# Norms of q and k: from the start of each mixing tile into the projections

## What is computed

```python
qkv, dn_conv_new = causal_conv(dn_qkv, dn_conv_prev, dn_conv_w)
qkv = jax.nn.silu(qkv)
q, k, v = jnp.split(qkv, [DN_QK_DIM, 2 * DN_QK_DIM], axis=-1)
q = l2_normalize(q.reshape(bsz, length, DN_HEADS, DN_HEAD_K)) * (DN_HEAD_K ** -0.5)
k = l2_normalize(k.reshape(bsz, length, DN_HEADS, DN_HEAD_K))
v = v.reshape(bsz, length, DN_HEADS, DN_HEAD_V)
beta = jax.nn.sigmoid(dn_b.astype(jnp.float32))
o, dn_s = run_segments(gated_delta_chunked, (q, k, v, g, beta), dn_s0, n_lead)
```

## Time and profile before

| | |
|---|---|
| three timed runs, us | 5544.49, 5547.06, 5552.38 (median 5547.06) |
| the profiled execution, us | 5531.47 |
| its span, first to last instruction, us | 5529.6 |
| mean granted clock of TensorE | 0.806 of full speed |
| busy share PE, DVE, POOL, ACT | 64%, 63%, 51%, 9% |
| HBM traffic | 278 GB/s over the span |
| A, B, C (from the first instruction of one stage to the next) | 0 to 284, 1036 to 1463, 2698 to 3237 us |
| openings of the mixing tiles 0 to 8 (L1492) | 292, 617, 1468, 1825, 2251, 3242, 3599, 4021, 4465 us |

### The profile page before, as it was taken

One profiled execution on the slowest core, in us unless ns is written; L12 is line 12 of the kernel. 1 busy time (PEld: TensorE's weight loads), 2 busy tenths in 40 slices (PEclk: granted clock), 3 DMA queues, 4 the chain that ended last, 5 costly groups with the idle time before them and its releaser, 6 DMA issues. The chain is left out here.

```text
span 5529.6 us, 50329 instructions
## 1 busy us (share of the span) xinstructions
PE 3563.1 (64%) x16620; PEld 2011.1 (36%) x16620; DVE 3470.3 (63%) x7379; ACT 472.4 (9%) x1615; POOL 2792.7 (51%) x2333
## 2 busy tenths in 40 slices
PE   6877366588886566576478888566656646566206
PEld 5564262244462452352133355154235222111001
DVE  3244995568554895676557644599568667685370
ACT  1110000011110000000021110000000000000000
POOL 1010465564443665775454433376577575425685
PEclk9988688699998778777699999777877866578558
DMA  4452468898767779889888756688989986759768
GB/s 165 132 177 101 176 218 295 308 369 295 279 208 297 263 248 361 330 312 343 295 326 302 277 189 231 250 296 277 362 320 322 347 306 225 277 199 371 258 216 304
DMA packets 467249, 1496.86 MB, mean 271 GB/s; under 512 B 60097, under 2 KB 122241, under 8 KB 454417
## 3 DMA queue, kind: packets, MB, share of 16 engines
q0 software_dynamic: 324864, 1141.04, 57.2%
q1 hardware_dynamic: 120912, 330.01, 16.2%
q10 hardware_dynamic: 21216, 22.60, 1.3%
HBM read 1480.07 MB, written 55.29 MB: 278 GB/s over the span
## 5 line engine op out<-in xcount | busy, mean ns | idle before, releaser
L1946 POOL DMA_INDIRECT e_ring<-peer_u,e_idx x1152 | 1462.2, 1269 | 1189.8 <-issue 515.1
L1946 POOL DMA_INDIRECT e_ring<-peer_v,e_idxT x1104 | 1190.6, 1078 | 1138.4 <-PE e_ff L2098 599.1
L1982 DVE CUSTOM_DVE_ANT_0 e_ring<-e_ring,e_x 128x1024 f32<-128x1024 f32 (+1 forms) x1152 | 1393.6, 1243 | 276.2 <-DMA e_ring<-peer_u,e_idx 269.7
L2098 PE MATMUL e_ff<-e_ring,e_strips 128*32 128x512 f32 x4416 | 756.8, 784 | 609.7 <-DMA e_ring<-peer_v,e_idxT 469.9
L349 PE MATMUL p_ps<-p_hT,p_w 128*128 128x256 f32 (+2 forms) x1728 | 568.8, 483 | 0.0
L2098 PEld LDWEIGHTS e_ff<-e_ring,e_strips 128*32 128x32 f32 x4416 | 165.1, 129 | 1097.7 <-issue 1094.6
L349 PEld LDWEIGHTS p_ps<-p_hT,p_w 128*128 128x128 f32 x1728 | 328.8, 195 | 205.6 <-issue 125.9
L1332 PE MATMUL bank<-wbuf,kqb 128*128 128x512 f32 (+1 forms) x576 | 302.1, 682 | 110.7 <-DMA wbuf<-w_out 110.6
L1184 PE MATMUL bank<-X,atp 128*128 128x128 f32 (+1 forms) x1632 | 240.9, 299 | 91.0 <-DVE XT L1525 58.9
L1365 PE MATMUL bank<-wbuf,kqb 128*128 128x512 f32 (+1 forms) x576 | 272.9, 623 | 20.8 <-DMA wbuf<-wc 20.7
L1193 PE MATMUL bank<-T,XT 128*128 128x128 f32 (+1 forms) x1344 | 209.8, 307 | 94.4 <-DVE T L1531 89.9
(11 more groups left out here) (323 smaller groups left out, 4147.7 us busy)
## 6 DMA issues: line engine op xcount, KB each, us to landing
p_w<-w_in SPq DMA_DIRECT2D x156, 512.0 KB, 3.6
wbuf<-w_out SPq DMA_DIRECT2D x72, 1024.0 KB
wbuf<-wc SPq DMA_DIRECT2D x72, 1024.0 KB
e_ring<-peer_u,e_idx POOLq DMA_INDIRECT x1152
e_ring<-peer_v,e_idxT POOLq DMA_INDIRECT x1104
rows<-p_tok SPq DMA_DIRECT2D x72, 192.0 KB
rows<-rows SPq DMA_DIRECT2D x8, 1280.0 KB, 9.0
z<-p_zs SPq DMA_DIRECT2D x32, 256.0 KB
```

Of the source, the lines that this page charges most:

```text
L1946: g.indirect_dma_start(out=self.ring[:, i % RING, :], out_offset=None, in_=table[:, :], in_offset=at, bounds_check=NEXP - 1, oob_is_err=Fa ...
L1982: v.tensor_tensor_reduce(out=self.ring[0:U, i, :], in0=self.ring[0:U, i, :], in1=self.x[0:U, :], scale=1.0, scalar=0.0, op0=ALU.mult, op1= ...
L2098: last = nc.tensor.matmul(self.ff[i][32 * j:32 * j + 32, :], self.strips[:, self.strip_of[t] % NSTRIP, j, 31 - s:63 - s], self.ring[:, sel ...
```

## The change

The sums of squares of the heads of q and k are taken in `project`, from the transposed blocks in `tok`, two blocks behind: at block j VectorE sums the squares of block j - 3 and squares block j - 2 (j from 2 to 18), ahead of the taps of block j. At block 20 it takes the root for all rows of the stage's tiles at once and writes three new groups of 16 columns beside the gates: `rq` (with the factor 1/8), `rk`, and `rkb` = rk times beta. The gates have 256 columns then instead of 208, and their store waits for `g_norms`. In `mix_tile` the squares, sums, root and scaling are gone; VectorE waits for the gates, makes kb from the raw k with `rkb`, waits for that, and then scales k and q in place. Nothing of the other engines' work is changed.

```diff
 for _n, _w in (("g", 2 * H), ("ncum", 2 * H), ("ecum", 2 * H), ("elast", 2 * H), ("beta", H), ("nbecum", H),
-               ("edl", H), ("dt", H), ("dtedl", H)):
+               ("edl", H), ("dt", H), ("dtedl", H), ("rq", H), ("rk", H), ("rkb", H)):
...
-                sp.wait_ge(S["g_done"], 1)
+                sp.wait_ge(S["g_norms"], 1)
...
+                squares = Chain(v, S["g_sq"])
+                squares.mark(v.memset(ssq[:], 1.0))
+
+                def squared(j):
+
+                    v.wait_ge(S["c_trevac"], NB * (j + 1))
+                    squares.sync()
+                    last = v.tensor_tensor(sq[:, 0:nf, :], tok[:, j % 2, 0:nf, :], tok[:, j % 2, 0:nf, :], ALU.mult)
+                    if packed:
+                        last = v.tensor_tensor(sq[0:PACK, nf, :], tok[0:PACK, j % 2, nf, :], tok[0:PACK, j % 2, nf, :], ALU.mult)
+                    squares.mark(last)
+
+                def summed(j):
+
+                    squares.sync()
+                    halves = lambda ap: ap.rearrange("p i (h d) -> p i h d", d=HD)
+                    last = v.tensor_reduce(out=ssq[:, 0:nf, 2 * j:2 * j + 2], in_=halves(sq[:, 0:nf, :]), axis=AX, op=ALU.add)
+                    if packed:
+                        last = v.tensor_reduce(out=ssq[0:PACK, nf, 2 * j:2 * j + 2], in_=sq[0:PACK, nf, :].rearrange("p (h d) -> p h d", d=HD),
+                                               axis=AX, op=ALU.add)
+                    squares.mark(last)
+
+                def norms():
+
+                    squares.sync()
+                    inverse_root(v, squares, ssq[:], ssx[:], ssw[:], ssq[:], 1.0, L2_EPS)
+                    v.wait_ge(S["g_done"], 1)
+                    v.tensor_scalar(F("rq"), ssq[:, :, 0:H], HD ** -0.5, None, ALU.mult)
+                    v.tensor_copy(F("rk"), ssq[:, :, H:2 * H])
+                    v.tensor_tensor(F("rkb"), ssq[:, :, H:2 * H], F("beta"), ALU.mult).then_inc(S["g_norms"], 1)
+
                 taps = Chain(v, S["c_taps"])
                 v.wait_ge(S["c_cst"], 32 if packed else 16)
                 for j in range(CT):
                     if j >= 2:
                         copy_out(j - 1)
+                    if 1 <= j - 2 < H + 1:
+                        summed(j - 3)
+                    if 0 <= j - 2 < H:
+                        squared(j - 2)
+                    if j == H + 4:
+                        norms()
                     v.wait_ge(S["c_evac"], j + 1)
...
                 v.wait_ge(S["qk_in"], 16)
-                c(tt(sq[0:R, :], q, q, ALU.mult))
-                c(v.tensor_reduce(out=B["ss"][0:R, 0:H], in_=heads(sq[0:R, :]), axis=AX, op=ALU.add))
-                c(tt(sq[0:R, :], k, k, ALU.mult))
-                c(v.tensor_reduce(out=B["ss"][0:R, H:2 * H], in_=heads(sq[0:R, :]), axis=AX, op=ALU.add))
+                v.wait_ge(S["gates_in"], 16)
                 at("norm")
-                root_of(B["rs"][0:R, :], B["ss"][0:R, :], 1.0, L2_EPS, 2 * H)
-                c(v.tensor_scalar(B["rs"][0:R, 0:H], B["rs"][0:R, 0:H], HD ** -0.5, None, ALU.mult))
-                tt(heads(q), heads(q), per_head(B["rs"][0:R, 0:H]), ALU.mult)
-                tt(heads(k), heads(k), per_head(B["rs"][0:R, H:2 * H]), ALU.mult).then_inc(S["qk_norm"], 1)
-                v.wait_ge(S["qk_norm"], 1)
-                v.wait_ge(S["gates_in"], 16)
-                tt(heads(kb[0:R]), heads(k), per_head(F("beta")[0:R]), ALU.mult).then_inc(S["kb"], 1)
+                tt(heads(kb[0:R]), heads(k), per_head(F("rkb")[0:R]), ALU.mult).then_inc(S["kb"], 1)
+                v.wait_ge(S["kb"], 1)
+                tt(heads(k), heads(k), per_head(F("rk")[0:R]), ALU.mult)
+                tt(heads(q), heads(q), per_head(F("rq")[0:R]), ALU.mult).then_inc(S["qk_norm"], 1)
```

More of the change, by code:

```diff
@@ L166, in project @@
         out = sb("p_out", [P, NT, NG])
+        sq, ssq, ssx, ssw = sb("p_sq", [P, NT, P]), *(sb(f"p_{n}", [P, NT, 2 * H]) for n in ("ssq", "ssx", "ssw"))
         ps = [ctx.enter_context(nc.psum_tensor(f"p_ps{i}", [P, 512], F32, allow_name_mangling=True)) for i in range(6)]
@@ L172, in project @@
                  "z_ws", "z_small", "z_mm", "z_silu", "z_st0", "z_st1", "z_st2",
-                 "g_in", "g_v", "g_mag", "g_e1", "g_p1", "g_ln", "g_decay", "g_sums", "g_last", "g_exp", "g_done", "g_store"] + [
+                 "g_in", "g_v", "g_mag", "g_e1", "g_p1", "g_ln", "g_decay", "g_sums", "g_last", "g_exp", "g_done", "g_store", "g_sq", "g_norms"] + [
                  f"w_in{i}" for i in range(NWR)]
@@ L928, in allocate_mix @@
             ("delta", [P, 512], F32), ("bct", [P, 4, P], F32), ("cb", [P, 2, P], F32),
-            ("ss", [P, 2 * H], F32), ("rs", [P, 2 * H], F32), ("root_x", [P, 2 * H], F32), ("root_w", [P, 2 * H], F32),
+            ("ss", [P, H], F32), ("rs", [P, H], F32), ("root_x", [P, H], F32), ("root_w", [P, H], F32),
             ("ssy", [P, 2], F32), ("stats", [P, 2, 6], F32), ("mv", [P, 4], F32),
```

## The result

The changed kernel is slower by 0.39% (ratio 1.0039, 95% interval 1.0025 to 1.0053; medians 5567.95 and 5547.26 us, 18 runs of each). A second measurement, beside other runs of the kernel before, gave 1.0033 (1.0015 to 1.0050; medians 5546.80 and 5534.17 us). So the change costs about 20 us by the ratios, and 20.7 and 12.6 us by the medians; the forecast was 9.4, 5556.5 us, "same". In brief: the projections cost in sum what the forecast said, though its terms for the clock missed both ways; tile 0 gained a little more than it said; and the other 8 to 12 us could not be placed.

What follows compares the result with a forecast made beforehand. No engine is full; a chain of stages with barriers bounds the kernel, each with its own last wait. Projections +15.0 less openings 5.6 gives +9.4 us on the 5547.06 median: 5556.5 us, range 5537 to 5568.

Steps and rivals of the forecast that it cites:

- What gates an opening: Mixing-tile openings: TensorE's first transposes wait for GpSimd's cast of `hidden` in six tiles (71.2 us), for kb only in tile 0.
- the last rival: Mixing tiles: the opening on VectorE heads every tile's chain, 64 us less and 15 more, 5498 us; chance 0.06.
- Tile 0: Opening of the first mixing tile, without gathers: TensorE starts at 300.5 in place of 305.08, gain 4.6 us.
- Tiles 1, 3, 6: Openings that begin with seven dots: `hidden` comes no sooner, masks gain 0.3 us each, 1.0 in all.
- The rival: Tiles 1, 3, 6: early dots hold back gathers and the cast, `hidden` later, +1 us each; chance 0.20.
- The projections: Squares and sums fit the slack of ordinary blocks; stalls at the root and block 17, with clock, cost 15.0 us.
- A: Projection for tiles 0 and 1, 256 columns: root 2.0 us over its slack plus 1.6 of clock, 3.6.
- B: Projection for tiles 2 to 4, 384 columns: 2.1 us at block 17 and 1.1 at the root, 3.2.
- C: Projection for tiles 5 to 8: 2.9 us stall plus 2.9 clock at block 17, 0.8 at the root, 6.6.
- Roots of B and C: At block 20 of these projections: 1.1 and 0.8 us over the slack, plus 1.6 of clock for one of the two.
- the projections hide it: Projections: the root's steps overlap more and no stall shows, only -5.6 us, 5541.5 us; chance 0.12.
- stalls and locks: Projections and tiles 1, 3, 6: each new idle lowers the clock, early dots delay `hidden`; +20.6 us, 5567.7 us; chance 0.20.

Runs made afterwards that it cites:

- Openings alone: New mixing-tile openings with the old projections, constants in place of the norms, against the kernel before: 1.0002, measured again 0.9981.
- the root behind the blocks: Changed kernel with the root and its three closing products behind the last block instead of at block 20: 1.0029 and 1.0016 against the kernel before.
- norms in A only: Kernel before with squares, sums and root (behind the blocks) in the first projection alone, new opening in tile 0 alone, 256 gate columns: 1.0002.

## Why the prediction missed

**What gates an opening: right.** The transposes of all tiles without token sums ahead still wait for `hidden`; kb went from the list of what ends the idle time. Openings alone measured 1.0002 and 0.9981, nowhere near the 64 us of the last rival.

**Tile 0: right, somewhat low.** TensorE starts 5.2 us sooner behind the tile's first load (4.6 forecast), and the tile is shorter by about as much: it took 319.6 us on average in twelve profiles of nine kernels with the new opening, 326.1 in four profiles of two kernels with the old one, 6.5 less. The size is loose: with the same old opening it took 327.4 and 328.1 us in the kernel before and 324.4 and 324.7 with the new projections, and another 2.7 us won at its opening brought nothing.

**Tiles 1, 3, 6: half right.** I took 0.3 us of gain each and left the lengthened gathers to a rival, because "early dots come one by one, as their rows land, with gathers between them". That step failed: dots and gathers did overlap, and the cast came 1.9, 1.4 and 1.3 us later in the changed kernel. The rival was right on the cast and wrong on what follows: VectorE's first masks came 0.8 to 1.8 us sooner all the same, and holding the dots back gained nothing. What all new openings of tiles 1 to 8 are worth is 5 us of cost, give or take 10; the forecast's gain of 1.0 lies inside. So this step had the overlap wrong, and no run shows that it cost time.

**The projections: right in sum and in the stalls, partly by luck in the clock.** Forecast 15.0 us; the stretches add up to 3.5 + 1.2 + 2.7 + 5.3 + 2.2 = 14.9 in the changed kernel and 1.9 + 1.1 + 2.7 + 5.7 + 2.2 = 13.6 in its second profile, against the first profile of before (A at block 20, B at 17 and 20, C at 17 and 20). The added idles were as forecast: 1.85, 1.04 and 0.53 us at the roots (2.0, 1.1 and 0.8), 2.25 and 3.04 at block 17 of B and C (2.1 and 2.9). What the clock added was not, and the misses cancelled.

A: 3.6 forecast, 3.5 and 1.9 seen (chain 1.85; the clock fell in one of the two). At block 17 of B the idle grew as forecast, but only 1.2 of it was left at block 19, since the slow products took 6.76 us instead of the 7.85 of before. Over more profiles the cost is larger: eight with B as before took 22.4 to 25.3 us for this stretch, nine with the squares 26.3 to 27.5, on average 2.7 more. C at block 17: 5.8 forecast, 5.3 to 5.9 seen. Roots of B and C: forecast 1.1 and 0.8, and 1.6 of clock for one of the two, 3.5; seen 2.7 and 2.2, the clock fell in both, 4.9. Over the seven profiles with a root at block 20 it fell in two in A, where the forecast counted on it, in five in B, and in all seven in C. This is the term that the record shows mis-sized: 1.6 for one of the two, in place of some 1.7 for each. Against the rival "the projections hide it" every kernel with the whole change in the projections speaks.

**The sum: too small, and why is only partly known.** The steps known to have failed are the clock behind the roots of B and C and the gathers held to lie between the dots. Neither accounts for the missing time: the first is offset by A and by block 17 of B, the second has no price in any run. 14.9 less 6.5 is 8.4 us, the forecast's 9.4; measured are 20 (0.36% as the mean of two measurements; 16.7 by the medians).

The whole stages A, B and C say what their blocks say: 1263.5 us in the four profiles with changed projections and root at block 20 in the first table, 1248.8 in the four with the old ones, 14.7. With 5 us (give or take 10) in tiles 1 to 8 that makes 13, against 14 to 29 and 8 to 28 us by the two timed measurements. So the term that may have been mis-sized is tiles 1 to 8, set at -1.0; I cannot show it.

The same gap stands elsewhere by the ratios: with the root behind the blocks the profiles leave +1.1, +5.6 and -6.5, nothing in sum, and the times were 1.0029 and 1.0016; the five measurements of kernels with a shorter tile 0 and projections that cost nothing should have lain near 0.9988 and have a mean of 0.9997. By the medians it is smaller: the root behind the blocks is then 8.1 and 5.4 us over the kernel before. None of their stages shows why. Two places stand out over all profiles, each found by looking through every stage and so perhaps by chance. Tile 7 took 454.8 us on average in the seven profiles with the root at block 20, and 448.2 in the other thirteen, with standard deviations of 4.3 and 4.6. The start of C took 123.5 us in the eleven profiles with the new openings ahead of it and 120.5 in the other nine (3.7 and 3.1). No experiment tests either, and the cause of the gap stays open.

The rival "stalls and locks" named 20.6 us and comes next to the time, but not by its own sum: it had 22.2 in the projections, where 14.9 were seen, and 3 in the tiles.

**What should have been seen.** The profile of before was a lucky one in tiles 1 to 8: 3948.1 us, the shortest of all twenty profiles here. I had measured its distance to the median (15.6 us) and still took "0.2%, 11 us" as what could be told, while placing a forecast of 9.4 just under that bound: with the terms as they were, the chance of "slower" deserved to be near that of "same".

## What to carry to other kernels

Work moved off an engine at a place where another wait ends last gains nothing, and where it is put down its price is read block by block: the slack there, and what else has already used it up (here one block of 36, where an expert tile is normalized, made nearly all of the cost beside the root). A chain of dependent small steps belongs where nobody waits for it; put behind the loop the root cost nothing in the blocks. A stage's length in one profile is no evidence for a few us: profile the same program twice first, and compare distances between the same two instructions, which here repeated to 0.1 us, once 0.2, as long as the clock did not change, while a whole stage differed by up to 12 between two profiles of one kernel.

## What the runs showed of the hardware

- The same idle of TensorE ends at either clock. Behind 2.69 us in A the granted clock fell in two of seven profiles (products of 5.03 and 5.07 us instead of 3.62), behind 2.07 to 2.09 us at block 20 of B in five of seven (7.02 instead of 5.33), behind 2.10 to 2.18 us in C in all seven (7.58 to 8.09 instead of 6.39); behind 3.13 us at block 17 of B the products took 7.85, 7.02 or 5.33 us in kernels that are alike up to there. The second profile of the kernel before (its first stands in the earlier trace rows, with 7.85 us):

```profile
1264.18 0.55 PE L333 MATMUL p_ps<-ident,p_sil 128*128 128x128 f32 x3 [3.13 <-ACT p_sil L425]
1264.56 7.02 PE L349 MATMUL p_ps<-p_hT,p_w 128*128 128x384 f32 x16
```

  and the kernel with norms in A only, whose B is that of before (granted clock 1.00 from 1246 to 1251 us, against 0.68 on average from 1264.6 to 1270 in the one above):

```profile
1245.60 0.55 PE L334 MATMUL p_ps<-ident,p_sil 128*128 128x128 f32 x3 [3.14 <-ACT p_sil L426]
1245.98 5.33 PE L350 MATMUL p_ps<-p_hT,p_w 128*128 128x384 f32 x16
```

- Idles of 4.69 to 4.72 us at block 17 of C were followed by slow products in all nine profiles that had them (8.27 to 8.87 us against 6.39), so there the price of a stall is the stall plus 2.3 to 2.9 us, the slower transposes (1.11 against 0.66) included.
- A longer idle can cost less clock: in B 5.39 us of idle were followed by 6.76 us of products, 3.14 by 7.85, so half of the added stall came back at once. It is no rule: two of the nine profiles with the longer idle had 7.82 and 7.84 us behind it.
- In tile 1 of the changed kernel the gathers that GpSimd issued beside VectorE's dots took 1.14 to 1.82 us, most others 0.99; one beside the product for kb took 1.41, so the dots are not alone in it. With the dots held back, the last five ahead of the cast took 0.99 again.
